# A selected-attention layer made one phase of 32 heads in turns with its weight steps, scores a turn ahead, and a fourth early item in mixing

## What is computed

```python
q, kc, vc, ks, vs, kw, vw, gate = jnp.split(h @ w_in, splits, axis=-1)   # 16 heads of 64, 4 groups of keys and values
kc_b = compress_kv(to_kv(kc), cmp_pos[0], cmp_w1[0], cmp_w2[0])          # 15 blocks of 32 tokens: gelu(flat @ w1) @ w2
vc_b = compress_kv(to_kv(vc), cmp_pos[1], cmp_w1[1], cmp_w2[1])
s_cmp = jnp.einsum("bsgrd,bngd->bgrsn", q, kc_b) * scale
p_cmp = masked_softmax(s_cmp, cmp_end[None, :] <= t[:, None])
o_cmp = jnp.einsum("bgrsn,bngd->bsgrd", p_cmp, vc_b)
n_sel = min(SLC_TOPK, n_slc)                                             # 4 blocks of 64 keys, all are selected
o_slc = selected_block_attention(q, to_kv(ks), to_kv(vs), sel_idx, rel_table)
o_win = banded_attention(q, to_kv(kw), to_kv(vw), rel_table, B_WINDOW)   # window 512 > 256: causal
g = jax.nn.sigmoid(gate)
o = g[..., 0:1] * o_cmp + g[..., 1:2] * o_slc + g[..., 2:3] * o_win
return o.reshape(B, S, -1) @ w_out
```

## Time and profile before

| | us |
|---|---|
| lowest of three runs | 3489.97 |
| median | 3492.57 |
| highest | 3493.9 |
| the profiled execution | 3493.43 |
| its span, first instruction to last | 3491.4 |
| of this: PE busy | 3354.4 |
| DVE busy | 2099.4 |
| ACT busy | 1717.0 |

### The profile page before, as it was taken

One profiled execution on the slowest core, in us unless ns is written; L12 is line 12 of the kernel. 1 busy time (PEld: TensorE's weight loads), 2 busy tenths in 40 slices (PEclk: granted clock), 3 DMA queues, 4 the chain that ended last, 5 costly groups with the idle time before them and its releaser, 6 DMA issues. The chain is left out here.

```text
span 3491.4 us, 53492 instructions
## 1 busy us (share of the span) xinstructions
PE 3354.4 (96%) x20376; PEld 2964.8 (85%) x20376; DVE 2099.4 (60%) x2315; ACT 1717.0 (49%) x2279; POOL 81.5 (2%) x180
## 2 busy tenths in 40 slices
PE   8999999999999999999999998899999999999899
PEld 6889988888999888887888888788888888888787
DVE  5567565555665555566565564655656655656655
ACT  4456544444554544455444442444445544445544
POOL 0000000000000000000000000100000000000000
PEclk9999999999999999999999987999999999999999
DMA  6656444555544454553545542254545445545354
GB/s 248 216 205 214 143 181 180 193 183 190 193 167 150 181 193 178 183 185 137 185 179 195 190 152 90 74 191 180 193 180 192 159 169 182 191 181 195 130 190 171
DMA packets 105214, 618.78 MB, mean 177 GB/s; under 512 B 10832, under 2 KB 19152, under 8 KB 34800
## 3 DMA queue, kind: packets, MB, share of 16 engines
q1 hardware_dynamic: 84288, 562.07, 44.1%
q10 hardware_dynamic: 20784, 54.71, 4.5%
HBM read 615.62 MB, written 9.50 MB: 179 GB/s over the span
## 5 line engine op out<-in xcount | busy, mean ns | idle before, releaser
L1292 DVE TENSOR_TENSOR wlo<-raw,whi 128x2048 fp32r<-128x2048 f32 x526 | 1204.5, 2291 | 668.2 <-ACT whi L761 666.0
L1983 PE MATMUL ps<-xhl,whi 128*128 128x512 f32 x3456 | 1201.9, 396 | 0.0
L761 ACT CAST whi<-raw 128x2048 fp32r<-128x2048 f32 x526 | 1001.6, 1904 | 199.7 <-PE ps L2119 108.9
L1987 PE MATMUL ps<-xhl,wlo 128*128 128x256 f32 x3456 | 893.1, 279 | 0.0
L1983 PEld LDWEIGHTS ps<-xhl,whi 128*128 128x128 f32 x3456 | 626.5, 188 | 121.8
L1987 PEld LDWEIGHTS ps<-xhl,wlo 128*128 128x128 f32 x3456 | 651.5, 189 | 37.5
L2118 PE MATMUL ps<-wlo,ht 128*128 128x512 f32 x1056 | 417.1, 395 | 0.0
L2117 PE MATMUL ps<-whi,ht 128*128 128x512 f32 x1056 | 417.1, 395 | 0.0
L2119 PE MATMUL ps<-whi,ht 128*128 128x512 f32 x1056 | 416.6, 394 | 0.0
L2098 PE MATMUL ps<-xhl,whi 128*128 128x256 f32 x1360 | 395.6, 291 | 11.1 <-DVE qb L1702 4.5
L2099 PE MATMUL ps<-xhl,whi 128*128 128x256 f32 x1360 | 390.2, 287 | 0.0
(11 more groups left out here) (299 smaller groups left out, 3940.7 us busy)
## 6 DMA issues: line engine op xcount, KB each, us to landing
raw<-stream SPq DMA_DIRECT2D x528, 1024.0 KB, 4.8
bias<-rel_bias ACTq DMA_DIRECT2D x80, 256.0 KB, 2.6
gain<-gains ACTq DMA_DIRECT2D x19, 1024.0 KB, 4.7
bias<-fixed_bias ACTq DMA_DIRECT2D x40, 256.0 KB, 3.6
rel_bias<-rel_vectors SPq DMA_DIRECT2D x16, 512.0 KB
x<-x_tokens ACTq DMA_DIRECT2D x1, 1024.0 KB, 5.0
y_tokens<-x ACTq DMA_DIRECT2D x1, 1024.0 KB, 3.9
s<-constants ACTq DMA_DIRECT2D x1, 512.0 KB, 6.6
```

Of the source, the lines that this page charges most:

```text
L761: nc.scalar.copy(whi[:, slot, :], raw[:, slot, :]).then_inc(sem["hi_ready"], 1)
L1292: nc.vector.tensor_tensor(wlo[:, slot, :], raw[:, slot, :], whi[:, slot, :].bitcast(F32), ALU.subtract).then_inc(sem["lo_ready"], 1)
L1983: wide = lambda: pe.matmul(ps[:, bank, 0:2 * half], hi[:, k, col0:col0 + P], src[:, k0 + k, :], start=first and k == 0, stop=last and k == ...
L1987: e = pe.matmul(ps[:, bank, 0:half], lo[:, k, col0:col0 + P], src[:, k0 + k, 0:half], start=False, stop=False)
```

## The change

**The selected layer is one phase, `nsa`.** A list of items (`nsa_items`) holds its weight steps in a new order and the parts of the compressed branch; the weight stream on the host is put in the same order. Four items stand ahead of the turns (v, q, k, gate), then 32 heads go in 34 turns, in groups of eight: four selected and four windowed heads of the same query heads. `NSA_SLOTS` says how many parts stand in each turn. `NSA_TURNS` says in which turn which of the eight pairs of heads is transposed; it begins at turn 23. The phases project, compress, cmp_attend, attend, turn and wout are gone, with their phase waits and their fillers; after the layer `between` has 18 fillers where it had 5.

```diff
+    items = [one("v", 0, 4, "act"), one("q", 0, 5, "dve"), one("k", 0, 6, "dve"), Item("gate", 0, 1, (7,), 2, "act"),
+             one("cmp", 0, 4, "act"), one("cmp", 1, 5, "act"), one("k", 4, 6, "dve"), one("v", 256, 7, "act"),
+             one("q", 4, 4, "dve"), Item("hidden", 0, 2, (5, 6), 4, "dve"), one("q", 8, 7, "dve"),
+             Item("hidden", 1, 2, (4, 5), 4, "dve"), one("q", 12, 6, "dve"), Item("blocks", 0, 0, (4,), 1, "act"),
+             Item("cmp_scores", 0, 0, (7,), 1, "dve"), Item("cmp_turn", 0, 0, (5, 6), 1, "act"), Item("cmp_values", 0, 0, (7, 4), 1, "add"),
+             Item("cmp_values", 1, 0, (5, 6), 1, "add")]
+    items += [Item("out", i, 1, (), 4, "") for i in range(4)]
...
+NSA_EARLY = 4
+NSA_HEADS = 2 * HEADS
+NSA_SLOTS = slots_of([(n, part) for n in range(NSA_EARLY, len(NSA) - 1) for part in range(NSA[n].parts)][:-1],
+                     [4, 4, 4, 3, 3, 2, 2, 2, 2, 2, 2, 1, 1, 2, 3, 0, 1, 0, 0, 1, 1, 1, 0, 0, 0, 2, 2, 2, 2, 1, 1, 1, 0, 0])
+NSA_TURNS = {23: 0, 24: 1, 25: 2, 26: 3, 27: 4, 28: 5, 31: 6, 33: 7}
+NSA_GELU = 13
+NSA_ADD = 22
```

PE's turns, and those of DVE:

```diff
+                scores(0)
+                for t in range(ph.n + 2):
+                    if t + 1 < ph.n:
+                        scores(t + 1)
+                    if 1 <= t <= ph.n:
+                        turn_probs(t - 1)
+                    if t in NSA_TURNS:
+                        turn_heads(NSA_TURNS[t], t)
+                    for n, part in NSA_SLOTS[t]:
+                        part_of(n, part)
+                    if 1 <= t <= ph.n:
+                        values(t - 1)
+                for i, quarter in ((3, 0), (3, 1), (2, 3), (3, 2), (3, 3)):
+                    out(i, quarter)
...
+                for t in range(ph.n + 2):
+                    if t == NSA_ADD:
+                        compressed_added()
+                    if 2 <= t <= ph.n + 1:
+                        heads_out(t - 2)
+                    if t < ph.n:
+                        biased(t)
+                    if t in NSA_TURNS:
+                        turned(NSA_TURNS[t], 3)
+                    if 1 <= t <= ph.n:
+                        inverted(t - 1)
+                    follow(NSA_SLOTS[t])
```

```diff
-WEAVE_TURNS = {5: 0, 7: 1, 9: 2, 11: 3, 13: 4, 15: 5, 17: 6, 18: 7}
-GQA_SLOTS = slots_of([part for j in range(3, 8) for part in quarters(j)][:-1], [1] * 19)
+WEAVE_TURNS = {3: 0, 5: 1, 7: 2, 9: 3, 11: 4, 13: 5, 15: 6, 17: 7}
+GQA_SLOTS = slots_of([part for j in range(3, 8) for part in quarters(j)][:-1],
+                     [2, 2, 1, 1, 1, 1, 1, 1, 1, 1, 1, 1, 1, 1, 1, 1, 1, 0])
 MOBA_SLOTS = slots_of([part for j in range(4, 15) for part in quarters(j)][:-1],
-                      [2, 2, 2, 2, 3, 3, 3, 3, 3, 3, 3, 3] + [2, 2, 2, 2, 1, 1, 1])
+                      [3, 3, 3, 3, 3, 3, 3, 3, 3, 3, 3, 2] + [2, 2, 1, 1, 1, 1])
```

```diff
-MIX_EARLY = 3
+MIX_EARLY = 4
...
-                     [5] * 10 + [4] * 14)
+                     [5, 5, 5, 5, 5, 4, 4, 4, 4, 4, 5, 4] + [4] * 12)
```

More of the change, by code:

```diff
@@ L211, in ends_item, with step_of, begins_step, emptied @@
-def ends_item(n, part):
-    return part == MIX[n].parts - 1
-def emptied(n, by):
-    return sum(item.by == by for item in MIX[:n])
+def step_of(items, n, part):
+    return items[n].step + part * items[n].steps // items[n].parts
+def begins_step(items, n, part):
+    return items[n].steps > 0 and part % (items[n].parts // items[n].steps) == 0
+def ends_item(items, n, part):
+    return part == items[n].parts - 1
+def emptied(items, n, by):
+    return sum(item.by == by for item in items[:n])
@@ new lines, in place, with nsa_items @@
+def place(items, kind, at=0):
+    return next(n for n, i in enumerate(items) if (i.kind, i.at) == (kind, at))
+def nsa_items():
+    one = lambda kind, at, bank, by: Item(kind, at, 1, (bank,), 4, by)
+    items = [one("v", 0, 4, "act"), one("q", 0, 5, "dve"), one("k", 0, 6, "dve"), Item("gate", 0, 1, (7,), 2, "act"),
[5 more added lines that the diff above has]
+    items += [Item("out", i, 1, (), 4, "") for i in range(4)]
+    step = 0
+    for item in items:
+        item.step = step
+        step += item.steps
+    return items, step
@@ L1083, in high_heads @@
                         nc.scalar.copy(v[:, :, 512:512 + P], ps[:, bank, T:2 * T].rearrange("p (t c) -> p t c", t=TT))
-                    for rows, other, q, k, heads, nt in heads_of(item):
+                    for rows, other, q, k, heads, nt in heads_of(item, ph):
                         made = ps[rows, bank, 0:nt * T].rearrange("p (i t) -> p i t", i=nt)
@@ new lines, in turned, with follow @@
+                def turned(k, bank):
+                    dve.wait_ge(sem["hi_made"], B["hi_made"] + k + 1)
+                    nc.vector.tensor_tensor(br2[:, k, T:2 * T], ps[:, bank, 0:T], br2[:, k, 0:T].bitcast(F32), ALU.subtract)\
+                        .then_inc(sem["lo_made"], 1)
+                def follow(parts):
+                    for n, part in parts:
+                        if begins_step(NSA, n, part):
+                            ahead(ph, step_of(NSA, n, part))
+                        if ends_item(NSA, n, part):
+                            empty(n)
@@ new lines, in nsa @@
+                for n in range(NSA_EARLY):
+                    ahead(ph, NSA[n].step)
+                    empty(n)
+                for t in range(ph.n + 2):
+                    if t == NSA_ADD:
+                        compressed_added()
+                    if 2 <= t <= ph.n + 1:
+                        heads_out(t - 2)
+                    if t < ph.n:
+                        biased(t)
+                    if t in NSA_TURNS:
+                        turned(NSA_TURNS[t], 3)
+                    if 1 <= t <= ph.n:
+                        inverted(t - 1)
+                    follow(NSA_SLOTS[t])
```

1028 lines of the change are left out of this document (499 added, 529 removed).

## The result

The changed kernel takes 3532.1 us (median of four, 3530.0 to 3533.1) against 3491.9 for the kernel before: 1.0113 of its time, 95% interval 1.0098 to 1.0128. It is 40 us **slower**; the forecast was 89 us faster, 3404. The profiled execution has a span of 3531.3.

The account below looks back on a forecast made before the run. PE was taken to set the time, busy 3354 of 3491 us, so only its idle, filler or low-clock time could be saved. Savings of 55 (selected), 17 (mixing) and 17 (interleaved) made 89: 3492.6 to 3404, range 3370 to 3440.

Parts of the forecast that it names:

- Interleaved layers: Two gqa2 layers and moba: waits for `brw` and some others go, 5, 7 and 5 us less, together 17.
- Mixing: Both mixing stages: an early q step covers PE's wait before scores 0 and the low clock after; 17 us less together.
- the optimistic bound: One mixing stage: 11 us less, if the 2.2 us wait for qb's low parts goes too; 8.5 was taken.
- Selected layer: The merged stage: 218 us in place of 273, 55 less; bounds 185 and 245.
- The wait in turn 3: Selected layer: PE stands about 4 us after DVE's low parts of k and compressed blocks; profile: turn 3 or 4.
- stretch 2: Selected layer, turns 0 to 14: seven weight steps, hidden products and 15 heads, 78 us on PE, 86 with waits.
- stretch 3: Selected layer, turns 15 to 24, no weight step: latency sets the turns, plus compressed scores and softmax chain; 48 us.
- stretch 4: Selected layer, turns 25 to 31: 11 out quarters, 7 heads and about 2 us of waits; 28 us.
- DVE and the low clock in the selected layer: Rival: DVE and the low clock hold the merged stage at 240 us, run time 3426; chance 0.21.
- The term of 13.7 us: Selected layer, turns 0 to 14: the 128 hidden products priced at the full clock; 27.4 us was the other end.
- The "slower" rival: Rival: PE stays at 1.2 GHz in all the merged stage's turns, stage 332 us, run time 3518; chance 0.02.
- no gain: Rival: interleaved and mixing layers gain nothing, only the selected layer does, run time 3437; chance 0.07.

Follow-up runs that it names:

- e4: Changed kernel with ACT's high part of the split ahead of the exponentials in the selected layer only: 3515.6 us, layer 238.3 in place of 254.8.
- e6: e5 plus five filler transposes in each of the selected layer's turns 15 to 20, 23 and 24: 3431.1 us, layer 224.6.
- e9: e5 with both the fillers of e6 and the wide hidden products of e8: 3424.0 us, layer 224.7.
- e12: e9 with the compressed branch's softmax chain on DVE cut in two over turns 16 and 17, in five rounds: 3423.7 us, layer 222.0.
- e1: Changed kernel with the interleaved layers' turn order, tables and bank as before: 3456.6 us, 0.9897 of the kernel before.
- e2: Changed kernel with ACT's high part of the split ahead of the exponentials in the interleaved layers only: 3476.6 us.
- e5: Changed kernel with interleaved layers as before and ACT's split ahead of the exponentials in the selected layer: 3433.9 us, layer 232.0.
- e8: e5 with both kinds of hidden products widened to 240 columns from 120 and 60: 3430.5 us, layer 224.6.

## Why the prediction was wrong

**Interleaved layers: this step failed, in its sign.** It says that bias t "needs only DVE itself and the values of t-2", and of a split that it "loads DVE with 2.2 + 2.29", so that outputs start 1.5 late. It priced the three layers at 5, 7 and 5 us less; they took 21.4, 30.1 and 23.0 more. The split was counted as work of DVE and not as a wait of DVE. The split's high part had been moved behind the exponentials on ACT, the exponentials need DVE's maximum of the same turn, and the outputs of the turn stand behind the split on DVE: a chain over three engines in each turn in which a step begins, 3.15 us of idle DVE in the row above. The order excerpts ahead of the prediction showed PE's and DVE's rows; ACT's, where the swap stands, I read and gave no price. Second, the transposes of a pair in turn t now wait for the outputs of head t-2, whose values PE made in the turn just before (they share bank 3 with the values), where before they took heads up to t-4, in the last turn t-3; the prediction put the wait for the pair behind the quarters' products and overlooked that the transposes stand ahead of them. The experiments put 48 us on the first alone, 18 on all the rest of the change in these layers, and 75 on both together. How much of the 18 is this second step is not shown.

**Mixing: right.** 17.9 us less against 17. Scores 0 start without a wait, and no low stretch follows. The sum also holds terms that the forecast didn't have: a wait of 1.3 us for ACT's `gate`, at 348.73 in the profile of before, is gone in both, and behind the longer wait for `qb` the first has a new stretch of 3.4 us at 0.50. Of the two, the first gave 7.3 and the second 10.6, where I had halved the clock's part for the second. The wait for qb's low parts, whose going was the optimistic bound, is still there, 3.27 us in the first and 2.08 in the second:

```profile
300.65 0.39 PE L2081 MATMUL ps<-xhl,whi 128*128 128x256 f32 x1 [3.27 <-DVE qb L1573]
```

**Selected layer: 254.8 for 218.** By stretches, with the granted clock:

```profile
2018.80:2049.00 30.20, 28.64 (x217) 27.08 (x217) 22.61 (x23) 18.73 (x25) 2.84 (x5) 0.94 0.54 192
2049.00:2160.90 111.90, 98.85 (x673) 96.61 (x672) 66.76 (x117) 54.88 (x117) 0.95 (x1) 0.79 0.42 146
2160.90:2217.70 56.80, 43.92 (x222) 40.90 (x223) 30.77 (x85) 19.34 (x63) 0.00 (x0) 0.63 0.17 51
2217.70:2257.10 39.40, 31.76 (x161) 27.05 (x160) 21.79 (x48) 17.09 (x43) 0.00 (x0) 0.85 0.34 114
2257.10:2273.60 16.50, 13.84 (x62) 10.92 (x62) 5.37 (x13) 4.65 (x14) 2.60 (x6) 0.79 0.00 0
```

The forecast's terms were 28, 86, 48, 28 and 14, with 14 for the clock in all. The lead is right but for the clock. The wait in turn 3 was forecast at about 4 and measured at 4.70; it stands before scores 4 and is released by DVE's low parts of `k` themselves, not by DVE's outputs, as the forecast of the profile had it. What is under-sized is stretch 2 by 26 us, stretch 3 by 9 and stretch 4 by 11. Two causes:
- The order of ACT's split again. Putting it right took 16.5 us off (e4), 13 of them idle time of PE. This one is shown by an edit.
- The clock. I allowed 14 us for it, and this is the term that was mis-sized most. The layer spent 112 us of its 255 at 0.50, and PE was busy 217 us where the forecast's own sum at the full clock was 173: an estimate of 44 us for the clock, of which less shows in the layer's time where PE had time to spare. In stretch 2 the two hidden items span 16.7 and 16.4 us, the heads between their halves included, where e6 has 9.4 and 11.6 at the full clock: 12 us, and these count in full. In the thin turns low clock cost little, as the fillers of e6 and e9 show. In stretch 3 the compressed scores, forecast at 7 and 3 more for the clock, took PE 13.7 us and kept DVE waiting 12.95 us, until 2181:

```profile
2181.02 0.66 DVE L1818 TENSOR_SCALAR scmp<-ps 128x480 f32<-128x480 f32 x1 [12.95 <-PE ps L2609]
...
2184.42 0.66 DVE L1826 TENSOR_TENSOR scmp<-scmp,cst 128x480 f32<-128x480 f32 x1 [0.67 <-ACT scmp L1166]
...
2186.64 0.66 DVE L1834 TENSOR_TENSOR pcmp<-scmp,small 128x480 f32<-128x480 f32 x1
2187.33 0.48 DVE L1913 SCALAR_TENSOR_TENSOR o<-ps,small,o 128x64 f32<-128x64 f32 x2
```

The softmax chain is 6.3 us from first to last instruction (6.2 forecast), PE's wait 3.96 behind it (about 5 forecast). With e9's edits the layer takes 224.7 at a mean clock of 0.87, near the forecast, and with the chain cut in two 222.0 (e12). No run reached 218.

**The rivals.** The first, DVE and the low clock in the selected layer, named the low clock that came there and stopped at 240; DVE was busy 147 of the 255 us, so it didn't hold the stage by its load. The rule of the Trainium skill ("TensorE: Matmul & The Clock Gate", Part 1) that was weighed against the row says that idle time brings the throttle back and activity releases it. In the changed kernel's own profile the rule looks better than I judged: the first 7.3 us of the second hidden item ran at 1.00 until PE stood 2.27 us for values, and what came behind the wait at 0.50; the whole first item, behind waits of 1.92 and 1.28 us, ran at 0.50:

```profile
2098.40:2115.10 16.70, 16.70 (x81) 16.70 (x79) 9.86 (x16) 6.97 (x13) 0.00 (x0) 0.50 0.35 123
2127.60:2134.90 7.30, 7.25 (x64) 6.91 (x62) 3.89 (x9) 3.95 (x8) 0.00 (x0) 1.00 0.31 101
```

But e1, e2 and e4 don't agree with it: there the clock fell inside the second item with PE busy and no wait ahead, so idle time alone doesn't account for the falls. The hidden products did run at 1.00 throughout in e6, and in none of the nine profiles with the narrow ones did the clock rise inside an item once it had fallen. My reading of the one row of before saw only the second of these. The term of 13.7 us for them measured 23.5 us of busy PE in the changed kernel and 15.2 in e6, so its full-clock price was 1.5 too low and its clock was the larger error. The "slower" rival put the loss in the selected layer's clock, with a chance of 0.02; the true one was in the layers that I priced by what their waits named, and no rival looked at a new chain there. The range to 3440 had its upper end from "no gain", though a reordering of three engines can lose as much as it gains: a bound of -2 us a layer for gqa2 was given without a row for it.

## What to carry to other kernels

In a kernel where several engines work in turns, price a reordering by following each chain through every engine's queue, and give a moved step the price of what now waits behind it on its own engine and on the next: one exchange of two ACT steps of 1.9 and 1.0 us cost 48 us in three layers. Where, as here, two results take turns in one PSUM bank, the program makes each wait for the other, so ask how many turns old the data is that a step asks for. And when a merged stage loses its fillers, ask of each stretch at the low clock whether PE sets the time there: in the dense hidden turns it cost 7 us, while 10 us less of it in the thin turns gave 0.7.

## What the runs showed of the hardware that I had not expected

- The hidden products went from 0.21 us each at clock 0.50 (27.4 us for 128, before) to 0.12 at 1.00 (7.5 us for 64, e6), and 240 columns took no longer than 120 and 60: 9.5 us against 9.4 for the first item with its heads.
- The clock can fall while PE is busy without a break: in e4 after 3.6 us of hidden products at 1.00, with no wait over 0.15 us in the 32 us before, and in e1 and e2 after 3.3 and 3.5 us.
- The clock differs from run to run: the same narrow products, in kernels that are alike up to them, ran at 0.56 (e5) and at 1.00 (e6), 15.0 us against 9.4; the four runs of e5 spread over 7 us.
- Fillers of 128 columns, five a turn, cut a low stretch of 34 us to 27, and gave 0.5 us (e6 against e5) and 0.7 us (e9 against e8) from the second hidden item to the layer's end.
